# A decoder block with attention, convolution and expert mixer: loads of the second table's activations on another queue, and attention's scores behind probabilities times values

## What is computed

```
z    = x @ W_in                      # q | k | v | conv B, C, h | two gates
a    = attention(q, k, v, sinks) @ W_attn_out    # 32 query heads, 4 key heads, window 128
c    = (B * conv3(C * h)) @ W_conv_out
x    = LN(alpha * x + (sigmoid(g_a) * a + sigmoid(g_c) * c) @ W_o)
# expert mixer: 8 heads, each picks 16 of 128 x 128 experts
q    = x @ W_q; two top-16 searches per head, then the best 16 of their sums -> expert, gate
u    = u_tab[expert]; act = gelu(x . u); y = sum(gate * act * v_tab[expert])
x    = LN(alpha * x + y)
```

## Time and profile before

| | us |
|---|---|
| median of three runs | 3757.84 |
| lowest and highest of them | 3747.99, 3764.73 |
| the profiled execution | 3746.34 |
| its span, first to last instruction | 3744.5 |
| TensorE busy in it | 3707.9 |
| DVE busy | 2761.7 |
| ACT busy | 1404.5 |
| GpSimd busy | 1102.9 |

### The profile page before, as it was taken

How to read it: one execution, slowest core, us unless ns; L and a number is a source line. 1 busy time by engine, 2 the same in 40 slices (tenths; PEclk the granted TensorE clock), 3 DMA queues, 4 the chain that set the end, 5 groups by cost and what they waited for, 6 DMA issues and landing times.

```text
span 3744.5 us, 56023 instructions
## 1 busy us (share of the span) xinstructions
PE 3707.9 (99%) x22023; PEld 3312.7 (88%) x22023; DVE 2761.7 (74%) x3457; ACT 1404.5 (38%) x2039; POOL 1102.9 (29%) x579
## 2 busy tenths in 40 slices
PE   9999999999999999999999999999999999999998
PEld 8888888888987888888888899999999987888887
DVE  5655566566698665656565798899998878899889
ACT  5644444444335100000000134466665444444443
POOL 0000000000745323544453273323332214354431
PEclk9999999999999999999999999999999999999999
DMA  5345555555599999999999768999999999999996
GB/s 195 119 168 187 187 183 190 182 189 192 197 365 421 421 422 416 408 400 405 399 395 387 302 251 347 405 383 396 400 390 408 408 350 403 407 400 416 400 415 258
DMA packets 196692, 1232.58 MB, mean 329 GB/s; under 512 B 20336, under 2 KB 37312, under 8 KB 54976
## 3 DMA queue, kind: packets, MB, share of 16 engines
q1 hardware_dynamic: 110720, 656.51, 45.4%
q0 software_dynamic: 73728, 536.90, 34.9%
q10 hardware_dynamic: 12096, 37.23, 2.5%
HBM read 1193.34 MB, written 36.70 MB: 328 GB/s over the span
## 4 chain that ended last, share of the span: by engine, by line
PE 92%; DVE 5%; DMA 2%; issue 1%; ACT 0%; DVEq 0%; SPq 0%; ACTq 0%
PE dense_ps L1072 25%; PE dense_ps L1075 11%; PE dense_ps L1057 9%; PE dense_ps L1058 9%; PE dense_ps L1059 9%; PE dense_ps L1332 7%; PE dense_ps L1077 5%; PE score_ps L1332 4%; PE dense_ps L1105 3%; PE o_ps L1332 2%; PE oT_ps L1332 2%; PE dense_ps L1111 2%; PE score_ps L1294 2%; DMA wbuf<-in_peer_v_dram 1%; DVE h L1409 1%; PE score_ps L1180 1%
## 5 line engine op out<-in xcount | busy, mean ns | idle before, releaser
L1457 DVE TENSOR_TENSOR w_three<-wbuf,w_three 128x1024 fp32r<-128x1024 f32 x792 | 961.7, 1222 | 435.0 <-ACT w_three L640 434.3
L640 ACT ACTIVATE w_three<-wbuf 128x1024 fp32r<-128x1024 f32 x848 | 891.2, 1059 | 1004.4 <-DMA wbuf<-in_peer_v_dram 256.1
L1057 PE MATMUL dense_ps<-act_two,w_three 128*128 128x256 f32 x2752 | 788.0, 286 | 3.3 <-DVE w_three L1457 3.1
L1058 PE MATMUL dense_ps<-act_two,w_three 128*128 128x256 f32 x2752 | 780.1, 283 | 0.0
L1059 PE MATMUL dense_ps<-act_two,w_three 128*128 128x256 f32 x2752 | 779.9, 283 | 0.0
L1072 PE MATMUL dense_ps<-x2T,wbuf 128*128 128x256 f32 x3136 | 687.0, 380 | 0.0
L1072 PEld LDWEIGHTS dense_ps<-x2T,wbuf 128*128 128x128 f32 x3136 | 593.0, 190 | 90.7 <-issue 11.5
L587 POOL DMA_INDIRECT row<-in_peer_v_dram,expert x203 | 417.5, 2057 | 856.1 <-DVE h L1409 820.8
L1404 DVE SCALAR_TENSOR_TENSOR row<-row,h 128x2048 f32<-128x2048 f32 x256 | 574.8, 2286 | 74.8 <-DMA row<-in_peer_u_dram,expert 73.8
L587 POOL DMA_INDIRECT row<-in_peer_u_dram,expert x256 | 440.4, 1720 | 589.9 <-DVE row L1404 530.1
L1057 PEld LDWEIGHTS dense_ps<-act_two,w_three 128*128 128x128 f32 x2752 | 529.7, 192 | 15.2 <-issue 11.9
(11 more groups left out here) (294 smaller groups left out, 4315.0 us busy)
## 6 DMA issues: line engine op xcount, KB each, us to landing
wbuf<-in_w_units_dram SPq DMA_DIRECT2D x456, 1024.0 KB
wbuf<-in_peer_v_dram SPq DMA_DIRECT2D x126, 1024.0 KB
gate_spill<-gbuf ACTq DMA_DIRECT2D x8, 2048.0 KB
e_gate<-gate_spill SPq DMA_DIRECT2D x32, 512.0 KB
act_spill<-stage ACTq DMA_DIRECT2D x60, 256.0 KB, 8.9
e_act<-act_spill SPq DMA_DIRECT2D x30, 512.0 KB
row<-in_peer_u_dram,expert POOLq DMA_INDIRECT x256
row<-in_peer_v_dram,expert POOLq DMA_INDIRECT x203
```

The source lines that it names most:

```text
L640: act.activation(hi_of(n)[j // 2][:, j % 2, :], w_of(n)[j // 2][:, j % 2, :], ACT.Copy).then_inc(w_hi_ready, 1)
L1057: nc.tensor.matmul(out, w[0], x[0], start=opens, stop=False)
L1058: nc.tensor.matmul(out, w[0], x[1], start=False, stop=False)
L1457: V.tensor_tensor(lo_of(n)[j // 2][:, j % 2, :], w_of(n)[j // 2][:, j % 2, :], hi_of(n)[j // 2][:, j % 2, :].bitcast(F32), ALU.subtract).t ...
```

## The change

Two independent parts.

In the stage of the second table, `load_e` leaves SP's program, but for group 2, and stands in ACT's: for odd m, behind the high half of the last quarter and ahead of `move_e`, for group m // 2 + 3. It waits for `e_lo_ready` of q - 1 there and issues the activations and the gates on ACT's queue. SP issued group q when unit 2q - 6 was finished; ACT issues it when unit 2q - 5 is finished.

In attention, the scores of s + 2 are computed behind probabilities times values of s, in place of the scores of s + 1 behind the transposes of s. The scores of step 1 move into the prologue, between the two parts of a dense half. `masks` of s + 2 stand late in DVE's iteration instead of `masks` of s + 1 at its head; the gathered rows of an iteration go in three parts instead of two. ACT's `exps` of s + 1 stand directly behind the copies of the transposed probabilities, with a wait of their own (`pT_ready`) that the probabilities of s have been transposed before they are overwritten.

```diff
@@ SP, the second table
             for g in range(4):
                 load(N_V + 2 + 2 * g)
-                load_e(3 + g)
...
                 for g in range(4, 8):
                     load(N_V + 2 + 2 * g, 8, i)
-                    load_e(3 + g, i)
                     load(N_V + 3 + 2 * g, 8, i)
             load(N_V + U_UNITS - 6)
-            load_e(GROUPS - 1)
@@ ACT
+            def load_e(q):
+
+                act.wait_ge(e_lo_ready, q - 1)
+                act.dma_start(e_act[q % 2][:, :, :].rearrange("p b t -> p (b t)"),
+                              act_spill[q:q + 1, :, :].rearrange("o p x -> (o p) x")).then_inc(e_in[q % 2], 16)
+                if q < GROUPS - 1:
+                    pair, of = (q + 1) // 2, slice(4 * ((q + 1) % 2), 4 * ((q + 1) % 2) + 4)
+                    act.dma_start(e_gate[pair % 2][:, of, :, :].rearrange("p c b t -> p c (b t)"),
+                                  gate_spill[of, :, pair:pair + 1, :].rearrange("c p o x -> p c (o x)")
+                                  ).then_inc(gates_in[pair % 2], 16)
@@ ACT, exps(s)
                     act.wait_ge(nmax_ready, s + 1)
+                    if s % 16:
+                        act.wait_ge(pT_ready, 2 * s)
@@ ACT, attention's iteration
+                        if t == 0 and u % 2 and u < 7:
+                            key_copy(u + 1)
+                        if u < 7 or t == 0:
+                            exps(s + 1)
                         if t == 0:
                             split_hi(m, 3)
-                            if u % 2 and u < 7:
-                                key_copy(u + 1)
                         else:
                             split_hi(m + 1, 1)
-                        if u < 7 or t == 0:
-                            exps(s + 1)
                         split_hi(m + 1, 2 * t)
@@ ACT, the second table's unit m
                     split_hi(n + 1, 3)
+                if m % 2 and m // 2 + 3 < GROUPS:
+                    load_e(m // 2 + 3)
                 if m == 0:
@@ TensorE
                 scores(16 * b, 0, 0)
-                half_T(q0 + 1, acts, 1)
+                half_T(q0 + 1, acts, 1, k1=8)
+                scores(16 * b + 1, 0, 1)
+                half_T(q0 + 1, acts, 1, k0=8)
...
-                        if t == 0:
-                            scores(s + 1, u, 1)
-                        elif u < 7:
-                            scores(s + 1, u + 1, 0)
                         if t == 0:
                             begin(m, 0, 0)
                         half_T(m, acts, t, k1=8)
...
                         last.then_inc(oT_ready, 1)
+                        if u < 7:
+                            scores(s + 2, u + 1, t)
                         half_T(m, acts, t, k0=8)
@@ DVE
                 denominators(16 * b)
+                masks(16 * b + 1, 0, 1)
...
-                        if t == 0:
-                            masks(s + 1, u, 1)
-                        elif u < 7:
-                            masks(s + 1, u + 1, 0)
...
-                        rows(n, 2 * t, 4)
+                        rows(n, 3 * t, 6)
                         if u < 7 or t == 0:
                             denominators(s + 1)
+                        rows(n, 3 * t + 1, 6)
...
+                        if u < 7:
+                            masks(s + 2, u + 1, t)
                         split_lo(m + 1, 2 * t)
-                        rows(n, 2 * t + 1, 4)
+                        rows(n, 3 * t + 2, 6)
```

## The result

| | median us | four runs each | ratio to before (95%) |
|---|---|---|---|
| before | 3753.58 | 3747.99 to 3764.73 | |
| changed | 3797.42 | 3794.78 to 3805.22 | 1.0119 (1.0104 to 1.0135) |

The change makes the kernel 44 us slower; the forecast was 10.9 us faster. The profiled span is 3793.0 us against 3744.5, 48.5 us more. The time is lost in the second table's stage; attention gains what was forecast.

What follows compares the result with a forecast made beforehand. TensorE, busy 3707.9 of 3744.5 us, was taken as the bound. Savings of 5.6 (array switches), 0.8 (a wait) and 4.5 us (loads) sum to 10.9: 3757.84 to 3746.9 us, chance 0.46, range 3733 to 3761.

Steps and rivals of the forecast that it cites:

- Attention: Both halves of attention: one array switch less in 28 iterations, 5.6 us, and one wait less, 0.8 us.
- Values to scores: TensorE in attention: scores directly behind values cost one ordinary array switch, so 0.20 us is saved per iteration (ends 0 and 0.40).
- Weights behind nothing on SP's queue: Second table's stage: weight loads no longer held behind gates' 512 small packets on SP's queue; 4.5 us gained.
- the cap: Second table's stage: the loads' part can give at most the 5.75 us of idle TensorE in the window 3110 to 3660.
- the surplus of 11.5 us: Whole kernel: median of the runs shown exceeds the profiled run by 11.5 us, place unknown, carried over unchanged.
- the second rival: Whole kernel: nearly free switch, all 5.75 us of idle and 4 us of stray waits go; 21.8 us gained, 3736.1 us, chance 0.14.
- Gates too late: Second table's stage, DVE's product: gates expected to land in about 18 us against some 20, so no wait was forecast.
- the third rival: Second table's stage: gates on a third queue come late, 1 us on the average of 29; +22.6 us, 3780.4 us, chance 0.10.
- Time given: Second table's stage: from ACT's split before the new issue to DVE's product at 3194.77, 17.5 us.
- Worst landing: Gates on ACT's queue beside two full ones: 512 packets in 22 us behind activations' 6 us, 28 us at worst.
- Expected landing: Gates on ACT's queue: about 18 us, between 3 and 28, as the two other queues are not full all the time.
- Price: Second table's stage: gates late by 1 us beyond some 20 us of landing, on the average of 29, cost +29 us.

Runs made afterwards that it cites:

- loads_only: Kernel before with only the loads' part: activations and gates on ACT's queue, a unit later, attention as before; 3802.21 us, ratio 1.0128.
- experiments 4 and 5: experiment 4, and loads_only with each gates load reading 512 KB in 128 packets of 4 KB instead of 512 (wrong gates multiplied); the latter 3743.92 us, ratio 0.9967.
- experiments 8 to 10: Changed kernel with activations and gates issued a unit earlier (3739.22 us); with gates two units earlier still, activations at the old time on SP (3742.55) or ACT (3742.30).
- experiment 4: Kernel before with activations and gates moved to ACT's queue but asked for at the old time, a unit earlier than in the changed kernel; 3741.55 us, ratio 0.9952.
- attn_only: Kernel before with only the attention part of the change, loads of activations and gates still on SP's queue; 3747.06 us, ratio 0.9987.

## Why the prediction was wrong

**Attention: right.** Values to scores is one ordinary switch. 14 iterations of the first half are 0.18 us shorter each (9.08 to 8.90) and 14 of the second 0.195 (10.26 to 10.065), against 0.20 forecast; the first transposes' wait is gone. At the 8000th matmul, behind both halves, the changed kernel is 6.0 us ahead (forecast 6.4), loads_only 0.3. The cover on DVE and ACT held: no wait of TensorE in attention, and the gathers followed, with a DMA share of 1.01 as before.

**Weights behind nothing on SP's queue: right in direction, its cause likely but not isolated, and sized too small.** The loads gain 12.7 and 10.4 us in experiments 4 and 5 by the medians, and 6 to 9 in 8 to 10 once attention's 6 are taken off, where 4.5 was taken out of 5.75 us of idle TensorE. What was mis-sized is the cap: it was read from one stretch of one profiled run. This stage varies from run to run, and before's profile was a good one; between it and experiment 4's profile the stage differs by 1.3 us only (699.00 and 697.70). But attn_only, whose last stage is the same code as before's, has 713 us of it instead of 699:

```profile
3028.00:3741.00 713.00, 695.16 (x3024) 569.22 (x3023) 617.74 (x445) 291.65 (x284) 261.44 (x100) 0.99 0.96 377
```

One stall of it has the form that the prediction described, a weight load that SP issues behind activations and gates (one load of layer norm parameters stands between, too, and its part was not told apart). SP's issue of the gates, the weight load in the chain that ended last, and TensorE's first matmuls behind the wait:

```profile
3092.44 0.43 SPq L492 DMA_DIRECT2D e_gate<-gate_spill  x1
...
3097.03 20.86 DMA wbuf<-in_peer_v_dram
...
3120.34 2.07 PE L1345 MATMUL dense_ps<-w_three,e_hi 128*128 128x512 f32 x4 [7.09 <-DVE w_three L1470]
```

The load takes 20.86 us, TensorE stands 7.09 us for it, and the clock in the window 3116 to 3122 is 0.57. Before's runs lie from 3740 to 3772 us, those of experiments 8 to 10 from 3737.7 to 3745.1. So the surplus of 11.5 us "at a place unknown to me" has its likely place here, as the second rival supposed of 4 us of it. The Trainium skill (DMA: Bandwidth & Descriptors, Issuing engines are not separate DMA queues) says that using several issuing engines saves issue time alone. Experiment 4, which issues the same loads at about the same time from ACT, gains 0.5% (0.9952, 0.9936 to 0.9968), more than that rule alone gives; the measurement decides here.

**Gates too late: the failed step.** The forecast put DVE's wait for the gates at nothing, because it expected a landing of about 18 us against a limit of some 20. Measured are 71.7 us of waiting on DVE, and on TensorE 38.6 us of idle time and 15.8 of slower matmuls. The mechanism stood there as the third rival, with the place of the wait, and only one chance in ten. Its terms:

- Time given, 17.5 us: right for the loads that are needed at once (18.1 in the median), though the product of the earlier trace rows at 3194.77 is an odd group's and waits for no new gates. Worst landing 28 us: measured 30.0 (27.45, 29.97 and 28.43 in the chain above).
- Expected landing "about 18, as the two others are not full all the time". The median is 20.2 over all loads and 22.6 over those needed at once. The reason given is the error: the DMA share is 1.01 from 3110 to 3660, so the others are full nearly all the time, which the prediction itself used to reason about the gain.
- More than that, the median was held against the limit, not the spread. 10 of the 13 loads needed at once took over 20 us. With a landing between 3 and 28 us and a limit of 20, part of the loads had to be late; the forecast treated it as all or none.
- Price, 1 us for each of 29: only 14 can be late, since every second load of gates has two units more. Measured are 71.7 us on 11 of them, 6.5 us each. TensorE's idle time grew by 38.6 us, so DVE's cover took about (71.7 - 38.6) / 11 = 3 us of each; the prediction said 2.
- Not priced at all: the clock at its lower level around a stall, 15.8 us of the stage's 54.4. And the relief for the weights is inside the 54.4 us too: from experiment 4 to loads_only, which differ in the lateness alone, it is 61 us.

The forecast for this rival was +22.6 us; measured is +43.8. The range left it out.

**Open.** Whether the missed DMA work behind each stall (41 and 225 GB/s in the windows above) costs time of its own, or lies inside TensorE's idle time, was not told apart. In the changed kernel 11 of 25 loads of gates take 8 to 16 us, among them such as were asked for in a stall, when the DMA falls empty (3221.04: 9.8 us); so stalls and landings depend on each other, and the loss per load is no constant. Why the sixteen engines finish one load up to several microseconds apart is open too.

## What to carry to other kernels

A small-packet transfer on a queue of its own can give its neighbours their turns back, and pays for it with its own latency: with every queue full, its landing is about its packets divided by the turns per microsecond (here 512 / 28 = 18 us, and the worst landing was 30.0). Before it is moved, work that out, add what stands ahead of it on the new queue, and hold the worst value against the time from issue to use. Read that time from the wait in the code, for each instance: here every second load had two units more. If it doesn't fit, ask earlier in the same edit, where the buffer allows it; here that was free (experiment 4).

When one term of a forecast rests on a resource being full, the same fullness has to be put into the rival's terms.

## What the runs showed of the hardware that was not expected

- With three queues at work, packets alternate about one to one, whatever their size: 26, 28 and 28 in one microsecond, at 51.3, 42.0 and 8.3% of the engines' time. The same 512 KB took 20.2 us (median) in 512 packets and 14.3 in 128.
- The last of a load's sixteen parts can land long after the others: 30.0 us behind the issue, the one before it 23.0 (the load of 3197.95).
- TensorE was idle for 7.07 us up to 3230.42. Its granted clock was 0.90 in the window from 3222, 0.53 in that from 3228 and 1.00 in that from 3234: a stall can cost more than its length. Over the stage this was 15.8 us beside 38.6 us of additional idle time.
- The spread of run times: 24 us in 28 runs of before, some 5 us in the 7 to 11 runs of each of experiments 8 to 10, beside them. Experiments 4 and 5 had 15 us in 6 runs and 14 in 10, so small packets ahead of weights are not all of it; what else is, was not looked for.
